# State space layer: the samples' tokens on 128 spaced rows, and all new sample states in one run per turn

## What is computed

```python
proj = u @ w_in                                   # gate z, x, B, C, dt
xc = silu(conv_b + sum(xpad[:, k:k+l] * conv_w[k] for k in range(4)))
dt = softplus(dt_raw + dt_bias); a = -exp(a_log)
# per chunk of q tokens (samples: q = 8, one chunk), 8 groups of 4 heads x 64, state 128
a_cum = cumsum(dt * a); seg = a_cum[t] - a_cum[s]
wts = einsum(C, B) * exp(seg, causal) * dt;  y_diag = wts @ x
xw = exp(a_cum[-1] - a_cum) * dt * x
states = einsum('bcsgn,bcsgjp->bcgjpn', B, xw)    # new state of each chunk
h = exp(a_cum[-1]) * h + states                   # the sample states are an output
y_off = (C @ h_prev) * exp(a_cum);  y = y_diag + y_off + d_skip * x
gz = rms_norm_per_group(y * silu(z)) * norm_g;  out = gz @ w_out
```

## Time and profile before

| | us |
|---|---|
| median of 3 runs | 2460.37 (2456.17, 2460.37, 2461.14) |
| profiled execution, span from first to last instruction | 2457.2 |
| mean granted clock of TensorE, share of 2.4 GHz | 0.994 |

### The profile page before, as it was taken

One profiled execution on the slowest core, in us unless ns is written; L12 is line 12 of the kernel. 1 busy time (PEld: TensorE's weight loads), 2 busy tenths in 40 slices (PEclk: granted clock), 3 DMA queues, 4 the chain that ended last, 5 costly groups with the idle time before them and its releaser, 6 DMA issues.

```text
span 2457.2 us, 50185 instructions
## 1 busy us (share of the span) xinstructions
PE 2421.8 (99%) x19713; PEld 2363.8 (96%) x19713; DVE 1856.6 (76%) x3053; ACT 1391.8 (57%) x2388; POOL 731.7 (30%) x672
## 2 busy tenths in 40 slices
PE   8999999999999999999999999999999999999998
PEld 8999999889999989999999999999999997999998
DVE  8979767988888888978876988875235438988875
ACT  7757553645555556757665767664222227767663
POOL 1222233444454532222223222224322321222222
PEclk9999999999999998999999999999999999999999
DMA  6677743123333325677665676763443334677762
GB/s 191 163 169 172 167 119 114 47 95 106 105 101 102 97 88 132 167 160 172 159 146 128 161 168 165 173 150 124 157 141 124 136 110 105 161 170 163 173 149 89
DMA packets 105558, 339.00 MB, mean 138 GB/s; under 512 B 13648, under 2 KB 17232, under 8 KB 87056
## 3 DMA queue, kind: packets, MB, share of 16 engines
q1 hardware_dynamic: 53808, 242.38, 30.0%
q0 software_dynamic: 51552, 93.87, 22.7%
HBM read 223.04 MB, written 19.32 MB: 99 GB/s over the span
## 4 chain that ended last, share of the span: by engine, by line
PE 92%; DVE 4%; DMA 1%; ACT 1%; issue 0%; SPq 0%; DVEq 0%; ACTq 0%
PE ps L1627 17%; PE ps L1625 17%; PE ps L1635 17%; PE ps L1523 7%; PE ps L1531 7%; PE ps L1524 7%; PE ps L1644 2%; PE ps L1645 2%; PE ps L1652 2%; PE ps L1966 1%; PE ps L1967 1%; PE ps L1968 1%; PE ps L1574 1%; DMA sb_lw<-sb_rawf 1%; PE ps L1564 1%; PE ps L1565 1%
## 5 line engine op out<-in xcount | busy, mean ns | idle before, releaser
L1627 PE MATMUL ps<-sb_ual,sb_hw 128*128 128x288 f32 x2240 | 612.8, 295 | 0.0
L1625 PE MATMUL ps<-sb_uah,sb_hw 128*128 128x288 f32 x2240 | 609.5, 295 | 0.2
L799 POOL DMA_DIRECT2D sb_lw<-sb_rawf x328 | 282.2, 866 | 961.6 <-ACT sb_lw L970 944.9
L1625 PEld LDWEIGHTS ps<-sb_uah,sb_hw 128*128 128x128 f32 x2240 | 420.9, 188 | 0.9 <-issue 0.7
L1627 PEld LDWEIGHTS ps<-sb_ual,sb_hw 128*128 128x128 f32 x2240 | 421.2, 188 | 0.0
L1635 PE MATMUL ps<-sb_uah,sb_lw 128*128 128x288 f32 x2240 | 384.8, 293 | 1.1 <-DMA sb_lw<-sb_rawf 1.0
L782 POOL TENSOR_TENSOR sb_wl<-sb_raw,sb_wh 128x1024 fp32r<-128x1024 f32 (+1 forms) x106 | 259.2, 2449 | 412.6 <-ACT sb_wh L939 399.0
L1523 PE MATMUL ps<-sb_uh,sb_wh 128*128 128x288 f32 x1360 | 374.2, 302 | 0.4 <-DVE sb_zs L2707 0.2
L1524 PE MATMUL ps<-sb_ul,sb_wh 128*128 128x288 f32 x1360 | 366.6, 296 | 0.0
L1635 PEld LDWEIGHTS ps<-sb_uah,sb_lw 128*128 128x128 f32 x2240 | 327.9, 188 | 2.3 <-DMA sb_lw<-sb_rawf 1.8
L1523 PEld LDWEIGHTS ps<-sb_uh,sb_wh 128*128 128x128 f32 x1360 | 255.7, 188 | 10.3 <-issue 7.0
(11 more groups left out here) (357 smaller groups left out, 5118.2 us busy)
## 6 DMA issues: line engine op xcount, KB each, us to landing
sb_lw<-sb_rawf POOLq DMA_DIRECT2D x358, 256.0 KB, 3.7
sb_rawf<-w_ffn_in SPq DMA_DIRECT2D x87, 1024.0 KB, 5.0
sb_rawf<-w_ffn_so SPq DMA_DIRECT2D x32, 1024.0 KB, 5.0
sb_raw<-w_ssd SPq DMA_DIRECT2D x64, 512.0 KB, 3.6
sb_raw<-w_att SPq DMA_DIRECT2D x40, 512.0 KB, 3.7
sb_rawf<-w_ffn_out SPq DMA_DIRECT2D x32, 384.0 KB, 3.1
sb_h<-state SPq DMA_DIRECT2D x8, 1024.0 KB, 4.9
ssm_sample<-sb_h SPq DMA_DIRECT2D x8, 1024.0 KB, 4.8
```

The costliest lines, as they stand in the source:

```text
L799: pool.dma_start(slot(lw, p), rawf[:, s % 2, i * BL:(i + 1) * BL], accum_op=ALU.add).then_inc(ld_in[i], 16)
L1625: pe.matmul(out, w[:, k * P:(k + 1) * P], high[k], start=begins and k == 0, stop=False, skip_group_check=True)
L1627: pe.matmul(out, w[:, k * P:(k + 1) * P], low[k], start=False, stop=False, skip_group_check=True)
```

## The change

The samples' x and B no longer go to the last 64 columns of `xc` but to `xsp` and `bsp`, 128 columns where sample b's 8 tokens stand at 16b to 16b + 7 and the rest is zero (cleared once by GpSimd). Their transposes so fill 128 rows, and 32 rows hold two samples. `tok` gets its sample rows through spaced copies of the three coefficient rows in `bt` (cleared by VectorE in place of `tok`). Masks, `xds`, `xws`, `sgs` and `cbs` have 128 rows; `bd` is 128 rows by 2 by 128. `states` then has four row groups with two samples each, and one run per turn does all eight samples in banks 4 to 7 (turn 7: 2, 3, 6, 7): in the loop after `ahead(4)`, in turn 7 between the two token sums. VectorE's four state adds stand together after the scaling, and `ahead(5)` changes place with `conv(g + 1, 2)`. The diff, with 8 spaces of indentation taken off and the allocations of tiles cut:

```diff
@@ -221,7 +221,8 @@
     wl0 = at("wl0", [P, UW], F32R)
-    bd = at("bd", [SMP, NB // 2, NST])
+    bd = at("bd", [P, 2, NST])
+    xsp = at("xsp", [P, 2, P])
     ysc = at("ysc", [P, 2 * HPG * PD])
...
@@ -398,6 +401,14 @@
+def spaced(ap):
+
+    return ap.rearrange("p (b s) -> p b s", s=2 * NS)[:, :, 0:NS]
+
+def samples_of(i):
+
+    return bsp[:, :] if i == 2 else xsp[:, i, :]
+
 def of_residue(ap, r):
@@ -545,9 +556,9 @@
-def state_bank(half, rg, last):
-
-    return ((2, 3), (6, 7))[half][rg] if last else 6 + rg
+def state_bank(rg, last):
+
+    return (2, 3, 6, 7)[rg] if last else 4 + rg
@@ -821,6 +832,8 @@
         pool.memset(cz[:, :], 0.0)
+        pool.memset(xsp[:, :, :].rearrange("p i r -> p (i r)"), 0.0)
+        pool.memset(bsp[:, :], 0.0).then_inc(rows_zero, 1)
@@ -1255,7 +1268,8 @@
                 nc.scalar.activation(smp(cz[:, :], 32)[:, :, 0:NS], new, ACT.Silu, bias=bias)
-            nc.scalar.activation(smp(xc[:, k, SEQ:TOK]), new, ACT.Silu, bias=bias).then_inc(xc_ready, 1)
+            dst = smp(xc[:, k, SEQ:TOK]) if k == 3 else spaced(samples_of(k))
+            nc.scalar.activation(dst, new, ACT.Silu, bias=bias).then_inc(xc_ready, 1)
@@ -1367,6 +1381,7 @@
         high_part(0, 8, U_GRP + 6, UW)
+        act.wait_ge(rows_zero, 1)
         gate_out(0, 0)
@@ -1779,7 +1794,7 @@
                 for i in range(3):
-                    ins = pe.transpose(ps[0:SMP, 4, rows(i)], xc[:, i, SEQ:TOK], ident[:, :])
+                    ins = pe.transpose(ps[:, 4, rows(i)], samples_of(i), ident[:, :])
                 ins.then_inc(t_mm, 1)
@@ -1789,7 +1804,7 @@
             pe.wait_ge(xs_done, g + 1)
-            pe.matmul(ps[0:SMP, 4, 0:SMP], xc[:, 2, SEQ:TOK], xc[:, 3, SEQ:TOK],
+            pe.matmul(ps[:, 4, 0:SMP], samples_of(2), xc[:, 3, SEQ:TOK],
                       start=True, stop=True).then_inc(cb_mm, 1)
@@ -1869,20 +1884,14 @@
-        def states(g, half, last=False):
-
-            if last:
-                pe.wait_ge(so_evac, g * 8 + 1)
-                if half:
-                    pe.wait_ge(y_evac, g * 2 + 2)
-            elif half == 0:
-                pe.wait_ge(y_evac, g * 2 + 2)
-            else:
-                pe.wait_ge(ss_evac, g * 4 + 2)
+        def states(g, last=False):
+
+            pe.wait_ge(y_evac, g * 2 + 2)
+            pe.wait_ge(*((so_evac, g * 8 + 1) if last else (gsqrt_ready, g + 1)))
             for k in range(2):
-                for rg in range(2):
+                for rg in range(4):
                     r = slice(32 * rg, 32 * rg + 32)
-                    ins = pe.matmul(ps[:, state_bank(half, rg, last), k * 256:k * 256 + 256], bd[r, 2 * half + k, :],
+                    ins = pe.matmul(ps[:, state_bank(rg, last), k * 256:k * 256 + 256], bd[r, k, :],
                                     xws[r, :, :].rearrange("p j d -> p (j d)"), start=True, stop=True)
@@ -1976,9 +1985,9 @@
             for c in range(CH + 1):
-                n = P if c < CH else SMP
+                tokens = src[:, rows(c)] if c < CH else bt[0:HEADS, rows(q)]
                 col = (q * (CH + 1) + c) * HEADS
-                ins = pe.transpose(ps[0:n, 4, col:col + HEADS], src[:, c * P:c * P + n], ident[0:HEADS, 0:HEADS])
+                ins = pe.transpose(ps[:, 4, col:col + HEADS], tokens, ident[0:HEADS, 0:HEADS])
         ins.then_inc(dtok_mm, 1)
@@ -2016,9 +2025,8 @@
             ahead(3)
-            states(g, 0)
             ahead(4, lambda: group_sums(g))
-            states(g, 1)
+            states(g)
             ahead(5)
@@ -2032,9 +2040,8 @@
         last_outputs(g)
-        states(g, 0, True)
         token_sums(g, 0)
-        states(g, 1, True)
+        states(g, True)
         token_sums(g, 1)
@@ -2632,8 +2639,8 @@
             V.scalar_tensor_tensor(t1, t0, -1.0, t0, ALU.mult, ALU.max).then_inc(dt_abs, 1)
-            V.memset(tok[:, :, :, :].rearrange("p q c h -> p (q c h)"), 0.0)
             V.tensor_copy(onr[:, :], ones[0:H2, :])
+            V.memset(bt[0:HEADS, 0:3 * P], 0.0)
             dve.wait_ge(dt_exp, 1)
@@ -2662,7 +2669,10 @@
             dve.wait_ge(coef_exp, 1)
-            V.tensor_tensor(t2, t2, t0, ALU.mult).then_inc(dtok_in, 1)
+            step(V.tensor_tensor(t2, t2, t0, ALU.mult))
+            for q, src in enumerate((acT, t0, t2)):
+                ins = V.tensor_copy(spaced(bt[0:HEADS, rows(q)]), smp(src[0:HEADS, SEQ:TOK]))
+            ins.then_inc(dtok_in, 1)
@@ -2672,8 +2682,7 @@
             v = ps[:, 4, 0:3 * (CH + 1) * HEADS].rearrange("p (q c h) -> p q c h", q=3, c=CH + 1)
-            V.tensor_copy(tok[:, :, 0:CH, :], v[:, :, 0:CH, :])
-            V.tensor_copy(tok[0:SMP, :, CH, :], v[0:SMP, :, CH, :])
+            V.tensor_copy(tok[:, :, :, :], v)
             step(V.tensor_copy(acT[:, :], acm[:, 0, :].bitcast(F32)))
@@ -2742,7 +2751,7 @@
             for j in range(HPG):
-                ins = V.tensor_scalar(sgs[:, j, :], ps[0:SMP, 4, j * SMP:(j + 1) * SMP], gtok[0:SMP, 0, CH, j:j + 1],
+                ins = V.tensor_scalar(sgs[:, j, :], ps[:, 4, j * SMP:(j + 1) * SMP], gtok[:, 0, CH, j:j + 1],
                                       0.0, ALU.subtract, ALU.min)
@@ -2774,11 +2783,11 @@
             for q, dst in ((1, xds), (2, xws)):
-                V.tensor_tensor(dst[:, :, :], ps[0:SMP, 4, 0:2 * P].rearrange("p (j d) -> p j d", j=HPG),
-                                gtok[0:SMP, q, CH, :].unsqueeze(2).broadcast_to([SMP, HPG, PD]), ALU.mult)
-            half = [SMP, NB // 2, NST]
-            V.tensor_tensor(bd[:, :, :], ps[0:SMP, 4, 2 * P:3 * P].unsqueeze(1).broadcast_to(half),
-                            maskb[:, :].unsqueeze(2).broadcast_to(half), ALU.mult).then_inc(xs_done, 1)
+                V.tensor_tensor(dst[:, :, :], ps[:, 4, 0:2 * P].rearrange("p (j d) -> p j d", j=HPG),
+                                gtok[:, q, CH, :].unsqueeze(2).broadcast_to([P, HPG, PD]), ALU.mult)
+            both = [P, 2, NST]
+            V.tensor_tensor(bd[:, :, :], ps[:, 4, 2 * P:3 * P].unsqueeze(1).broadcast_to(both),
+                            maskb[:, :].unsqueeze(2).broadcast_to(both), ALU.mult).then_inc(xs_done, 1)
             def states():
@@ -2804,7 +2813,7 @@
             dve.wait_ge(cb_mm, g + 1)
-            V.tensor_tensor(cbs[:, :], ps[0:SMP, 4, 0:SMP], masks[:, :], ALU.mult)
+            V.tensor_tensor(cbs[:, :], ps[:, 4, 0:SMP], masks[:, :], ALU.mult)
             V.tensor_tensor(cbm[:, :].rearrange("p (c q) -> p c q", c=CH), ps[:, 5, :].rearrange("p (c q) -> p c q", c=CH),
@@ -2815,7 +2824,7 @@
                 dve.wait_ge(es_done, g + 1)
-                V.tensor_tensor(sgs[:, :, :], sgs[:, :, :], cbs[:, :].unsqueeze(1).broadcast_to([SMP, HPG, SMP]),
+                V.tensor_tensor(sgs[:, :, :], sgs[:, :, :], cbs[:, :].unsqueeze(1).broadcast_to([P, HPG, SMP]),
                                 ALU.mult).then_inc(w_done, 1)
@@ -2855,8 +2864,8 @@
                 V.scalar_tensor_tensor(ysb[:, i, 0:SEQ], xc[:, i, 0:SEQ], dk, ps[:, 5 + i, :], ALU.mult, ALU.add)
-                ins = V.scalar_tensor_tensor(ysb[:, i, SEQ:TOK], xc[:, i, SEQ:TOK], dk,
-                                             sample_out(i), ALU.mult, ALU.add)
+                ins = V.scalar_tensor_tensor(smp(ysb[:, i, SEQ:TOK]), spaced(samples_of(i)), dk,
+                                             smp(sample_out(i)), ALU.mult, ALU.add)
                 ins.then_inc(y_evac, 1)
@@ -2865,19 +2874,18 @@
-            def sample_states(half, row_groups=(0, 1)):
-                dve.wait_ge(ss_mm, g * 2 + half + 1)
+            def sample_states(row_groups):
+                dve.wait_ge(ss_mm, g + 1)
                 for rg in row_groups:
-                    b = 4 * rg + 2 * half
+                    b = 2 * rg
                     dve.wait_ge(hm_done, g * 8 + b + 2)
-                    V.tensor_tensor(h0[:, b:b + 2, :], h0[:, b:b + 2, :], two(ps[:, state_bank(half, rg, last), :]),
+                    V.tensor_tensor(h0[:, b:b + 2, :], h0[:, b:b + 2, :], two(ps[:, state_bank(rg, last), :]),
                                     ALU.add).then_inc(ss_evac, 1)
...
                 V.tensor_tensor(zs[:, 0, :], zs[:, 0, :], zs[:, 1, :], ALU.add).then_inc(gsum_done, 1)
-                sample_states(0)
                 if first:
@@ -2892,7 +2900,7 @@
                                 v.unsqueeze(2).broadcast_to(each), ALU.mult).then_inc(gsum_done, 1)
-                sample_states(0, (0,))
+                sample_states((0,))
                 dve.wait_ge(gn_mm, g + 2)
@@ -2905,23 +2913,23 @@
             if not last:
-                sample_states(1)
+                sample_states(range(4))
                 ahead(4)
...
             if not last:
+                ahead(5)
                 conv(g + 1, 2)
-                ahead(5)
             else:
-                sample_states(0, (1,))
+                sample_states((1,))
                 for m in range(KD):
...
                     else:
-                        sample_states(1)
+                        sample_states((2, 3))
```

(22 more changed lines are left out.)

## The result

The changed kernel takes 2463.96 us (median of 20 runs, 2459.68 to 2468.27) against 2460.57 us (20 runs, 2455.32 to 2467.08): a ratio of 1.0015, 95% interval 1.0008 to 1.0021, or 2 to 5 us more. The profiled execution has a span of 2459.3 us (before 2457.2), the granted clock is 0.994 in both. 2464 was predicted.

A forecast was written before the change was run, and what follows sets the result against it. TensorE, busy 99% of the span, was taken as the bound. Set-up 0.3, first to second turn 0.3, six loop turns 2.4 and last turn 0.4 gave +3.4 on 2460.4: 2464 us, range 2453 to 2472.

The forecast's parts named there:

- One run of states: Each turn on TensorE: one run of 16 passes replaces two of 8, in four rounds, gaining 1.26 us.
- rival B: States run: weight loads of four row groups queue, the run takes 1.9 us, 0.88 more per turn; 2470 us, chance 0.13.
- Group sums: Fourth product ahead: TensorE comes early and waits for VectorE's sum of squares, losing 0.45 of the 1.26 us.
- Taps behind the last gate: Loop turn: taps moved behind the gate end 1.25 us later, delaying ScalarE's exp_cum; TensorE stalls 1.54 us at sample_decays.
- Rival A: Loop turns: the moved taps are not in the way, so the savings are kept; 2454 us, chance 0.27.
- The 128 rows: Samples' products in each turn: two changes of tile shape and their pauses go, saving 0.34 us (0 to 0.4).
- Loop turn +0.4, six +2.4: Loop turns: 0.74 us later from the stall less 0.34 saved gives +0.4 each, +2.4 us over six.
- Rival C: Loop turns: the new stall halves TensorE's clock; three of six turns hit 2469 us, all 2474; chance 0.17.
- First to second turn: Between turns one and two: VectorE bounds, decays start at 497.2 instead of 495.96, project_out waits; +0.3 us (-1.5 to +2).
- Set-up: Before the first decays: three added VectorE copies in state_coefs lengthen the path by 0.3 us (0 to +0.65).
- Last turn: Last turn: ScalarE, 0.5 us later against TensorE, delays its bt copy and conv_out; +0.4 us (-0.3 to +1.5).
- the second token sums start when ScalarE's squares are ready, and that does not move: Last turn: start at 932.25 stays fixed, so the one run's saving becomes a 1 us wait before the first token sums.

The follow-up runs named there:

- run_twice: order_by_turn with every run of states issued twice, the second writing the same values again; 2460.78 us, ratio 1.0003 to the kernel before.
- short_both: order_by_turn with GpSimd's weight subtractions beside gl and the add of squares cut to 64 columns in the loop's turns, leaving work out; 2450.54 us, ratio 0.9965.
- before_swapped: The kernel before with only the order swapped: ahead(5) before the taps conv(g + 1, 2); 2468.77 us, ratio 1.0033.
- adds_in_the_gap: order_by_turn with turn 0's four state adds on VectorE placed between the reciprocal and the scalings; 2457.19 us, ratio 0.9988 to the kernel before.
- run_by_group: order_by_turn with the two loops of a run of states exchanged, the row group outside; 2456.59 us, ratio 0.9987 to the kernel before.
- order_by_turn: The changed kernel with the taps before ahead(5) again in the loop's turns, but ahead(5) first in turn 0; 2456.99 us, ratio 0.9985 to the kernel before.
- split_before_gl: order_by_turn with GpSimd's weight subtraction beside gl in two pieces, the second after the taps, all work kept; 2455.31 us, ratio 0.9972 to the kernel before.

## Why the prediction was right, and where it was not

- **One run of states, 1.26 us.** Right, and rival B is refuted: a round of four row groups costs what a round of two did (1.08 us for 16 passes, 1.06 for 8; run_twice adds 0.86 for 16 more). B has the weight loads queue, 0.11 us each by the earlier trace rows; they do not: the run's first four loads in the kernel after, 0.18 us each, start within 0.02 us (TensorE's weight loads at 557.14), and the next four 0.11 us behind them.
- **Group sums, 0.45 us lost.** 0.42 by the starts, and 0.12 more since the first pass of the sums is longer after the stop: the second starts 0.35 us behind it, 0.24 before and in short_both (5.41 instead of 5.29 us to the next run).
- **Taps behind the last gate, a stall of 1.54 us.** Decays to `sample_decays` went from 7.66 to 9.21: 1.55. before_swapped shows it by itself, 1.55. Rival A (the taps are not in the way), which I had at 0.27, fell.
- **The 128 rows, 0.34 us.** The pause is gone; what they brought in all comes from short_both, where nothing waits: 45.84 - 44.14 = 1.70, less the run's 1.26 leaves 0.44. A little under-sized: from the first product of C by B to `back(1)` a turn of short_both takes 2.66 us against 2.89, which is 0.23 where 0.14 was priced, and at the samples' products it saves the 0.15 of the pause. The 128 rows were not tried by themselves. On VectorE the rows cost 0.01 us and the columns count: `xds` takes 0.41 us on 64 rows before and 0.42 on 128 after, with 256 columns in both, `bd` 0.67 us with 512 columns and 0.42 with 256.
- **Loop turn +0.4, six +2.4.** 66.45 to 66.85; from turn 1's `sample_decays` to turn 7's 398.72 to 401.09 us, +2.37.
- **Rival C, the clock.** After the six waits of 1.44 us no stretch at the lower level follows: the granted clock is 1.00 from 510 to 915 us. After the 3.07 us before the second turn's decays it does fall (TensorE by windows, for the earlier trace rows):

```profile
496.00:499.00 3.00, 2.56 (x6) 0.58 0.68 254
499.00:503.00 4.00, 4.00 (x18) 0.50 0.93 320
503.00:507.00 4.00, 4.00 (x31) 0.96 0.67 277
...
510.00:915.00 405.00, 394.73 (x3188) 1.00 0.30 96
```

  That is half clock (0.50) from 496.5 to 503.3, twice as long as before (3.4 us from 502.4). The prediction's 1.2 and 2.4 GHz are granted clocks of 0.50 and 1.00: in the timeline before, passes of 288 columns start every 0.24 us from 502.5 to 505.6, which is 1.2 columns a ns, and every 0.13 us ahead of that. But how long TensorE stood does not settle it, as rival C took it to: in adds_in_the_gap its one wait ahead of the fall is 1.25 us, shorter than the six that did nothing, and the granted clock falls all the same (0.56 over 497 to 500). What tells the two places apart, no run shows.
- **First to second turn, +0.3.** +0.29, but not by the way I gave: the decays came 0.9 us later (52.04 to 52.95 from the first decays), not 1.2, and no block of `project_out` waited for VectorE: at the lower clock TensorE was the later of the two (VectorE's taps end at 501.5, and its next add then stands 0.20 us for TensorE). The 0.29 is partly luck too. From the first decays to the second turn's `sample_decays` it is only +0.08 (63.62 to 63.70), for the stretch from the first decays to the first `sample_decays`, which I had not priced, was 0.20 shorter: the lower clock that falls there ended 0.5 us behind the first `sample_decays` in the kernel after, and ahead of them in the kernel before.
- **Set-up, +0.3.** From the start of VectorE's last product of the coefficients (430.97 before, 430.20 after) to the first decays 12.95 to 13.29 us, +0.34. VectorE's timeline after has the copies as priced (three from 430.98 to 431.30, 0.11 us each):

```profile
430.98 0.18 DVE L2674 COPY sb_bt<-sb_acT 32x64 f32<-32x64 f32 x1
431.09 0.28 DVE L2674 COPY sb_bt<-sb_er 32x64 f32<-32x64 f32 x2
```

- **Last turn, +0.4: not seen, and the step behind it failed.** `sample_decays` to the first output product went from 34.06 to 33.58, -0.48. The step that failed is "the second token sums start when ScalarE's squares are ready, and that does not move". Their row of before has no bracket: they waited for nobody, and moved 0.48 us earlier (26.00 to 25.52 behind `sample_decays`). ScalarE's delay was there (0.42 us up to the old states' product), and the wait of 1 us before the first token sums too (1.05 in the trace):

```profile
931.43 1.18 PE L1909 MATMUL ps<-sb_ones,sb_zs 128*96 128x1 f32 x12 [1.05 <-ACT sb_zs L1349]
932.54 1.32 PE L1894 MATMUL ps<-sb_xws,sb_bd 32*128 32x256 f32 x16
933.80 2.08 PE L1909 MATMUL ps<-sb_ones,sb_zs 128*96 128x1 f32 x12
```

  But the prompt's and the samples' outputs ahead of it were 1.05 us shorter from their first pass to the last `ident` product (922.82 to 928.53 before, 925.28 to 929.94 after), and that outweighed it. The pause of 0.15, gone twice, is 0.3 of it. The rest is where a stretch at half clock (0.50) falls: from 922.3 to 925.7 before, on these outputs; from 923.1 to 926.6 after, mostly on the old states' product, behind which TensorE would else have stood for VectorE. First before, then after:

```profile
920.77 1.07 PE L1843 MATMUL ps<-sb_h,sb_cz 128*32 128x256 f32 x16 [2.07 <-DVE sb_hst L2791]
922.82 1.17 PE L1853 MATMUL ps<-sb_sg,sb_xd 128*64 128x128 f32 x8 [0.98 <-DVE sb_sg L2814]
924.15 0.69 PE L1853 MATMUL ps<-sb_sg,sb_xd 128*64 128x128 f32 x4
```
```profile
923.22 1.94 PE L1858 MATMUL ps<-sb_h,sb_cz 128*32 128x256 f32 x16 [2.16 <-DVE sb_hst L2800]
925.28 1.18 PE L1868 MATMUL ps<-sb_sg,sb_xd 128*64 128x128 f32 x8
926.59 0.44 PE L1868 MATMUL ps<-sb_sg,sb_xd 128*64 128x128 f32 x4
```

  So 1.6 us less of the outputs is done at the lower clock, which at half the speed is 0.8 us by estimate. Where the stretch falls changes by itself: before_swapped has the last turn of the kernel before, line for line, and takes 35.11 us. So the sign of this term is not settled by one execution of each.

The sum over the mixer in the profiled executions is 0.34 - 0.20 (first decays to first `sample_decays`, not priced) + 0.29 + 2.37 - 0.48 = +2.3 us against +3.4 predicted; the medians differ by 3.4. That these two 3.4 agree is partly luck: the miss of the last turn lies within what the medians can tell, and the same code differs by 1 us at the first decays and again in the last turn from one profiled execution to another. The 2.4 of the six loop turns does not depend on that: the six turns agree within 0.08 us in the execution before and within 0.15 in the one after.

Where the gain went: TensorE saved 1.7 us in each of the six turns. Against it 0.55 was lost at the group sums and 1.55 at `sample_decays`, 2.1 in all, which is the 0.4 by which the turn grew. With the order put right 0.7 a turn stays, and with GpSimd out of VectorE's way (in a kernel that leaves work out) 1.7.

## What to carry to other kernels

When TensorE is 99% busy, a microsecond saved on it is only kept if the two or three chains that feed it were early by as much: list their slack at each place where TensorE needs them before pricing the saving. Never move an operation that TensorE waits for at a distance (taps, then silu, table load, exp) behind one that itself waits for TensorE: here that cost 1.55 us a turn (before_swapped). A row without a bracket says that nobody was waited for: what is saved ahead of it moves it. And the size of a gap is read from start to start against a dense pair, not from the bracket.

## What the runs showed of the hardware

- fp32 passes of 32 rows in four row groups ran at the cost of passes in two: 0.216 us a round of 256 columns, in either written order (after, run_by_group; before for two).
- A VectorE instruction with two tensors in SBUF that met a GpSimd subtraction already running ended 0.6 us behind that one's end: the sum of squares at 553.00 for 552.39 and the first `gl` at 565.18 for 564.56 (order_by_turn), the first scaling at 493.17 for 492.56 (after). So it took 1.51 instead of 0.75 us (short_both), two of `gl` 2.33 instead of 1.42 (short_both), the scalings 3.49 (after) instead of 1.54 (adds_in_the_gap). One with an operand in PSUM did not stand (adds 2.47 and 2.48 for four, GpSimd through or beside them). GpSimd's own subtraction takes 2.40 us in most places and 2.9 in the pair around the sum of squares (5.78 for two, order_by_turn); what stretches it no run isolates. Putting the two engines' work in another order frees VectorE without leaving work out (split_before_gl: `gl` 1.42 us again).
- Waits of 1.44 us, six times, left the granted clock at 1.00; one of 3.07 us was followed by 6.8 us at 0.50, and one of 1.25 us at the same place (adds_in_the_gap) by 3.4 us.
